# Splitting operands of five matrix products one stage ahead in a fused two-block kernel

## The reference, cut to what matters

```python
def conv_ffn(h, w_up, conv_w, conv_b, w_down):
    u = h @ w_up
    up = jnp.pad(u, ((0, 0), (1, 1), (0, 0)))
    u = up[:, :-2] * conv_w[0] + up[:, 1:-1] * conv_w[1] + up[:, 2:] * conv_w[2] + conv_b
    a, b = jnp.split(u, 2, axis=-1)
    return (jax.nn.silu(a) * b) @ w_down
...
        h = _rms(x, mix_norm_g[l])
        p = h @ w_in[l]
        a_out = _mla(...)
        kf = _hyena_filters(...)
        h_out = _hyena(p[..., OFF_HY:], hy_conv_w[l], hy_conv_b[l], kf, hy_skip[l])
        mixed = jnp.concatenate([_rms(a_out, attn_out_g[l]), _rms(h_out, hy_out_g[l])], axis=-1)
        x = x + mixed @ w_out[l]
        x = x + _mem_xattn(_rms(x, cross_norm_g[l]), _rms(mem, mem_norm_g[l]), w_mq[l], w_mkv[l], w_mo[l])
```

## Time and profile before

| what | value |
|---|---|
| median of 3 runs | 2826.53 us (2824.12 to 2827.61) |
| the profiled execution | 2820.73 us, span 2818.9 us |
| PE busy | 89% of the span |
| DVE, ACT, POOL busy | 49%, 30%, 9% |
| mean granted PE clock | 0.936 of full |

### The profile page before, as it was taken

One profiled execution on the slowest core, in us unless ns is written; L12 is line 12 of the kernel. 1 busy time (PEld: TensorE's weight loads), 2 busy tenths in 40 slices (PEclk: granted clock), 3 DMA queues, 4 the chain that ended last, 5 costly groups with the idle time before them and its releaser, 6 DMA issues. The chain is left out here.

```text
span 2818.9 us, 34789 instructions
## 1 busy us (share of the span) xinstructions
PE 2498.3 (89%) x14602; PEld 1936.7 (69%) x14602; DVE 1390.7 (49%) x2216; ACT 847.1 (30%) x1347; POOL 249.8 (9%) x180
## 2 busy tenths in 40 slices
PE   6997979999997998998799998998785889897887
PEld 5885658888886888985589996756533368573322
DVE  3324554666666115226657775356576645423223
ACT  4223443323224114224533333123401542221001
POOL 0002420000000000004300000000131020011112
PEclk8998989999998999997999998999897999988998
DMA  5114721111120112226322223211101013347996
GB/s 237 60 53 117 272 107 45 60 60 60 61 71 31 62 62 75 75 80 201 117 75 93 96 93 123 94 48 60 56 0 53 0 61 135 120 182 317 425 424 276
DMA packets 53949, 326.89 MB, mean 116 GB/s; under 512 B 7646, under 2 KB 13918, under 8 KB 25950
## 3 DMA queue, kind: packets, MB, share of 16 engines
q1 hardware_dynamic: 40750, 302.76, 28.7%
q0 software_dynamic: 5696, 12.59, 1.2%
q10 hardware_dynamic: 7344, 9.28, 1.0%
HBM read 317.26 MB, written 12.58 MB: 117 GB/s over the span
## 5 line engine op out<-in xcount | busy, mean ns | idle before, releaser
L947 PE MATMUL ps<-work_rounded,ring_rounded 128*128 128x512 f32 (+3 forms) x2128 | 576.3, 356 | 30.3 <-DVE work_rounded L395 13.1
L947 PE MATMUL ps<-xn_rounded,ring_rounded 128*128 128x512 f32 (+2 forms) x2304 | 545.0, 349 | 0.0
L2007 PE MATMUL ps<-xn_rounded,ring_rounded 128*128 128x258 f32 (+2 forms) x2816 | 533.9, 312 | 0.0
L2007 PEld LDWEIGHTS ps<-xn_rounded,ring_rounded 128*128 128x128 f32 x2816 | 413.4, 190 | 31.2
L947 PEld LDWEIGHTS ps<-work_rounded,ring_rounded 128*128 128x128 f32 (+2 forms) x2128 | 359.7, 193 | 92.7 <-DVE work_rounded L395 13.7
L947 PEld LDWEIGHTS ps<-xn_rounded,ring_rounded 128*128 128x128 f32 x2304 | 375.9, 192 | 58.0 <-issue 0.2
L947 PE MATMUL ps<-big_rounded,ring_rounded 128*128 128x512 f32 (+2 forms) x1160 | 337.4, 369 | 52.9 <-DVE big_rounded L854 43.7
L854 DVE TENSOR_TENSOR ring_rounded<-ring,ring_rounded 128x2048 fp32r<-128x2048 f32 (+2 forms) x94 | 189.0, 2015 | 254.5 <-ACT ring_rounded L822 254.4
L2007 PE MATMUL ps<-work_rounded,ring_rounded 128*128 128x256 f32 (+1 forms) x1232 | 279.6, 308 | 9.0 <-PEq L782 4.8
L947 PEld LDWEIGHTS ps<-big_rounded,ring_rounded 128*128 128x128 f32 (+1 forms) x1160 | 205.0, 196 | 95.9 <-DVE ring_rounded L854 32.3
L822 ACT ACTIVATE ring_rounded<-ring 128x2048 fp32r<-128x2048 f32 (+2 forms) x94 | 158.2, 1688 | 357.6 <-PE ps L947 351.7
(11 more groups left out here) (400 smaller groups left out, 3104.5 us busy)
## 6 DMA issues: line engine op xcount, KB each, us to landing
ring<-in_stream SPq DMA_DIRECT2D x141, 1024.0 KB, 4.8
big<-in_experts SPq DMA_DIRECT2D x22, 2048.0 KB, 29.3
ring<-in_stream SPq DMA_DIRECT2D x32, 704.0 KB, 3.9
ring<-in_experts SPq DMA_DIRECT2D x22, 1024.0 KB, 28.8
xn<-in_experts SPq DMA_DIRECT2D x5, 2048.0 KB, 30.4
work<-in_experts SPq DMA_DIRECT2D x5, 2048.0 KB, 35.5
big<-in_first_modulation SPq DMA_DIRECT2D x8, 1024.0 KB, 14.0
work<-in_bias ACTq DMA_DIRECT2D x24, 256.0 KB, 4.4
```

The costliest lines, as they stand in the source:

```text
L947: mm = pe.matmul(out[:, a - u.first:b - u.first], lhs, rhs, start=j == 0 and n == 0 and not u.onto, stop=j == terms - 1 and n == len(passe ...
L2007: mm = pe.matmul(out[:, a:b], ws[:, k, :], x[k][:, a - base:b - base], start=k == 0 and n == 0, stop=k == KT - 1 and n == 2)
```

## The change

Each of the five products gets part of its sources split in the stage before it. `project` takes `tiles_ahead`: the split order and PE's waits then start at that tile.

- `ffn_up` of the last layer splits tiles 0 to 8 of the down projection, one per tile of its own loop (ACT in half 1 of tile i for tile i-2, DVE for tile i-3), and at the last tile the first strip of the down projection. That strip's high part would fall on `high[0]`, which `ffn_up` uses for its own weights, so from here on the parity of the two areas is swapped (`turn`).
- `hyena_filters` splits 5 of the 8 tiles of `second_projection`: ACT after its exponentials, DVE between `take(0)` and `take(1)`. For this the hyena inputs lie in other columns of `work`.
- The latent attention splits the four hyena tiles of `mixed_projection`: ACT in units 10, 14, 18, 22, DVE in the unit behind.
- `mixed_projection` splits the 8 memory tiles of the memory projection: ACT after the square of units 0 to 7, DVE after these units.
- The memory attention splits 6 of the 8 tiles of `output_projection`: two by ACT in each of units 6, 10, 14, DVE in the unit behind.

```diff
+    def high_of(self, n):
+        return self.high[(n + self.turn) % 2][:, 0:WIDTH[n]]
...
-            for k in range(len(sources)):
+            for k in range(tiles_ahead, len(sources)):
...
-                            pe.wait_ge(tile_low.sem, tile_low.at(seen_tiles))
+                            if seen_tiles > tiles_ahead:
+                                pe.wait_ge(tile_low.sem, tile_low.at(seen_tiles - tiles_ahead))
@@ attention, vector and scalar @@
+                    for n, (at_unit, _, value, high) in enumerate(next_tiles):
+                        if u == at_unit + 1:
+                            dve.wait_ge(next_high.sem, next_high.at(n + 1))
+                            self.split_low(dve, value, high)
...
+                    for at_unit, outputs, value, high in next_tiles:
+                        if u == at_unit:
+                            act.wait_ge(stored.sem, stored.at(outputs))
+                            self.split_high(act, value, high).then_inc(next_high.up(), 1)
                     if pair_at(u, 2) is not None:
@@ ffn_up, scalar and vector @@
+                    if c == 1 and 0 <= i - 2 < tiles_ahead:
+                        act.wait_ge(gated.sem, gated.at(len(runs) * (i - 1)))
+                        self.split_high(act, *down_sources[i - 2]).then_inc(next_high.up(), 1)
+                    if (i, c) == (FT - 1, 0):
+                        for number, value, room in views():
+                            self.split_high(act, self.strip(act, number), room).then_inc(next_high.up(), 1)
...
+                    if c == 1 and 0 <= i - 3 < tiles_ahead:
+                        dve.wait_ge(next_high.sem, next_high.at(i - 2))
+                        self.split_low(dve, *down_sources[i - 3])
+                    if (i, c) == (FT - 1, 0):
+                        for _, value, room in views():
+                            dve.wait_ge(next_high.sem, next_high.at(tiles_ahead + 1))
+                            self.split_low(dve, value, room)
@@ hyena_filters, vector and scalar (PAIRED_AHEAD = 5) @@
+                take(0)
+                for k in range(PAIRED_AHEAD):
+                    dve.wait_ge(next_high.sem, next_high.at(k + 1))
+                    norm.low(dve, k)
+                take(1)
...
+                for k in range(PAIRED_AHEAD):
+                    if k == 3:
+                        act.wait_ge(multiplied.sem, multiplied.at(16))
+                    norm.high(act, k).then_inc(next_high.up(), 1)
@@ latent attention @@
+            next_tiles=[(10 + 4 * i, 1, mix[:, 4 + i, :], room) for i, room in enumerate(self.hyena_high())],
@@ mixed_projection @@
+            if i < KT:
+                memory_norm.high(act, i).then_inc(next_high.up(), 1)
...
+        def after(dve, i):
+            if i < KT:
+                dve.wait_ge(next_high.sem, next_high.at(i + 1))
+                memory_norm.low(dve, i)
@@ memory_attention @@
-        self.project(units, 12, finish, sources=rooms, deferred=norm, early=KT)
+        self.project(units, 12, finish, sources=norm.rooms, deferred=norm, early=KT, tiles_ahead=KT)
...
+            next_tiles=[(6 + 4 * (m // 2), 2 * (m // 2) + 2, o[:, m, :], self.output_high[m]) for m in range(6)])
```

More of the change, by code:

```diff
@@ L463, in on_tensor @@
             pe.wait_ge(b.hyena_landed, 64)
-            pe.matmul(b.bank(1)[0:64, :], b.v("w1", 0, 64)[0:33, :], b.work[0:33, 6144:6144 + S], start=True, stop=True).then_inc(self.done.up(), 1)
+            pe.matmul(b.bank(1)[0:64, :], b.v("w1", 0, 64)[0:33, :], b.work[0:33, 10240:10240 + S], start=True, stop=True).then_inc(self.done.up(), 1)
         if i == 4:
@@ L765, in __init__ @@
         self.issued = 0
-        self.ahead = 0
+        self.ahead = self.turn = 0
         self.freed_at = []
@@ L873, in project @@
     def project(self, units, strips, finish, sources, banks_each=1, prefetch=None, deferred=None, add=None, gpsimd=None,
-                early=None, following_strip=False, loads=None, following_halves=False, after=None, beside=None):
+                early=None, following_strip=False, loads=None, following_halves=False, after=None, beside=None, tiles_ahead=0):
         first = len(self.freed_at)
@@ L898, in parts @@
             low_w = [self.rounded(a) for a in slot]
-            high_w = [self.rounded(self.high[(first + s) % 2][:, 0:WIDTH[first + s]]) for s in strips_of_unit]
+            high_w = [self.rounded(self.high_of(first + s)) for s in strips_of_unit]
             low_x, high_x = ([self.rounded(t[part]) for t in sources] for part in (0, 1))
@@ L1005, in split_strip @@
                     else:
-                        ins = self.split_high(act, strip, self.high[(first + s) % 2][:, 0:WIDTH[first + s]])
+                        ins = self.split_high(act, strip, self.high_of(first + s))
                     ins.then_inc(strip_high.up(), 1)
@@ L1984, in ffn_up, with views @@
         halves_of = [(i, c) for i in range(FT) for c in range(2)]
+        down_sources, tiles_ahead = self.down_sources(l, width)
+        next_high = self.sig("next_high")
+        if not need_ctx:
+            self.turn = 1
+        def views():
+            return self.split_ahead(0 if need_ctx else 1)
         with self.stage() as block:
@@ L2090, in _, with down_sources @@
                         gate(i - 1)
+                    if c == 1 and 0 <= i - 3 < tiles_ahead:
[5 more added lines that the diff above has]
+                            self.split_low(dve, value, room)
                 convolve(*halves_of[-1])
                 gate(FT - 1)
+    def down_sources(self, l, width):
+        if l < DEPTH - 1:
+            rooms, ahead = tiles_in(width, self.xn, self.work), 0
+        else:
+            at = (FT + 1) * width
+            rooms = tiles_in(width, self.big[:, at:16384], self.xn, self.big[:, FT * width:at])
+            ahead = (16384 - at) // width
+        return [(self.g[:, k, :], room) for k, room in zip(range(FT), rooms)], ahead
     def ffn_down(self, l, need_ctx):
@@ L2106, in ffn_down @@
         last = l == DEPTH - 1
-        rooms = tiles_in(width, self.xn, self.big[:, FT * width:]) if last else tiles_in(width, self.xn, self.work)
-        self.project(units, 2 * KT, finish, banks_each=2, sources=[(g[:, k, :], room) for k, room in zip(range(FT), rooms)],
+        sources, tiles_ahead = self.down_sources(l, width)
+        self.project(units, 2 * KT, finish, banks_each=2, sources=sources, tiles_ahead=tiles_ahead,
                      following_strip=True, loads=self.load_hyena_inputs if last else None, beside=FilterFeatures(self) if last else None)
@@ L2235, in _ @@
                     combine(o)
-                for o in range(2):
-                    take(o)
+                take(0)
[3 more added lines that the diff above has]
+                take(1)
             @block.scalar
@@ L2254, in second_projection @@
     def second_projection(self):
[L2255 to L2256 removed]
+        p2, norm = self.bigs(0, 16, S), self.pair_norm
         self.p2 = p2
[L2258 to L2261 removed]
         units = []
@@ L2271, in finish, with paired_sources @@
             return eng.tensor_tensor(p2[0:n, i, :], ps, norm.rstd[0:n, :], ALU.mult)
-        self.project(units, 8, finish, sources=rooms, deferred=norm)
+        self.project(units, 8, finish, sources=norm.rooms, deferred=norm, tiles_ahead=PAIRED_AHEAD)
+    def paired_sources(self):
+        xn, w = self.xns(KT, S), self.work
+        rooms = [(w[:, 6144 + k * S:6144 + (k + 1) * S], xn[:, k, :]) for k in range(KT)]
+        areas = tiles_in(S, self.xn[:, 4096:6144])
+        self.first_rstd = w[:, 10240:10752]
+        self.both_gains = self.small[:, 96:104]
+        self.pair_norm = PairNorm(self, rooms, areas[0:2], areas[2:4], areas[1], self.first_rstd)
     def hyena(self):
@@ L2555, in add_squares, with memory_sources @@
                     settle(pool, pool.tensor_tensor(total, total, passes[(m - 1) % 3], ALU.add), added)
-        self.project(units, 4, finish, sources=rooms, deferred=OutputNorm(self, rooms, w[:, 7168:7680]), early=4, add=square, gpsimd=add_squares,
-                     following_strip=True)
+        memory_norm = self.memory_norm = self.memory_sources()
+        self.project(units, 4, finish, sources=rooms, deferred=OutputNorm(self, rooms, w[:, 7168:7680]), add=square, gpsimd=add_squares,
+                     following_strip=True, after=after, tiles_ahead=4)
+    def memory_sources(self):
+        xn, w = self.xns(KT, S), self.work
+        rooms = list(zip(tiles_in(256, self.big[:, 12288:14336]), tiles_in(256, self.big[:, 2048:4096])))
+        rooms += [(w[:, 2048 + k * S:2048 + (k + 1) * S], xn[:, k, :]) for k in range(KT)]
+        return MemoryNorm(self, rooms, self.memory, (self.memory_squares, self.stream_squares), (w[:, 8448:8704], w[:, 8704:9216]), self.small[:, 0:2])
     def memory_attention(self):
-        xn, hm, w = self.xns(KT, S), self.bigs(2048, KT, 256), self.work
```

(7 more changed lines are left out.)

46 lines of the change are left out of this document (24 added, 22 removed).

## The result

The changed kernel took 2806.7 us (median of 4 runs, 2805.9 to 2809.0), the kernel before, on the same chip, 2825.3 us (4 runs, 2824.1 to 2827.6). The ratio is 0.9935, with a 95% interval from 0.992 to 0.995. The gain by the medians is 18.6 us; 17.6 was forecast, and 2806.7 lies in the range and in the forecast's own range.

A forecast was written before the change was run, and what follows sets the result against it. PE, busy 89% of the span, was taken as the bound, standing at block starts for split operands. Gains 9.8 + 3.2 + 0.6 + 3.1 + 0.9 = 17.6 us: 2826.5 - 17.6 = 2808.9, range 2800 to 2818 (own 2804 to 2814).

The forecast's parts named there:

- The down projection: PE starts at about 1716.2, no longer waits for strip 1, and unit 0 ends at 1734.5: gain 9.8 us.
- The second projection: ACT and DVE lose five of eight tiles at its start, so everything behind moves up: gain 3.2 us.
- The mixed projection: Its head gains 3.1 us from wait and clock, four splits in the latent attention lose 2.5: net 0.6.
- rival 1: In the attention loops each of ten tiles delays PE in full: loss 11.4 instead of 4.7, time 2815.6; chance 0.12.
- The memory projection: Eight tiles split earlier let strip 1 and all behind move up: gain 3.1 us, moved work hidden in mixed projection.
- The output projection: Its head gains 3.1 us from wait and clock, six splits in the memory attention lose 2.2: net 0.9.
- The second: Down projection gains only its head, strip 1 or tables being late: 3.7 instead of 9.8, time 2815.0; chance 0.06.
- The third: More is gained: attention tiles cost nothing and the clock stays up: 2803 us or less; chance 0.12.
- The fourth: Whole kernel: no change in time because later waits swallow the gain, 2824 to 2829 us; chance 0.03.
- The fifth: Added waits in the attention loops make PE's clock fall and stay at 1.2 GHz: slower, 2849 us; chance 0.03.

The follow-up runs named there:

- e6: Kernel before's down projection tiles put back into the changed kernel, so only its first strip is split ahead there; other products as changed; 2816.03 us.
- e7: Changed kernel with only the nine tiles of the down projection split ahead, not its first strip; 2810.37 us.
- e10: The changed kernel unaltered, timed and profiled once more; 2809.24 us, ratio 0.994.
- e4: Changed kernel without the down projection's splits in `ffn_up`; the other four products stay split ahead; 2818.17 us, ratio 0.9971.
- e1: Changed kernel with the latent attention's four splits two units later, in units 12, 16, 20, 24; 2808.37 us, ratio 0.9937.
- e5: Changed kernel with splits moved: two each in latent attention units 15 and 23, and memory attention units 7, 11, 14; 2807.02 us, ratio 0.9944.
- e11: Same kernel as e5, run again on another chip, against the changed kernel's split places in both attentions; 2803.88 us, ratio 0.992.
- e12: Changed kernel with only the latent attention's splits moved, two each to units 15 and 23; 2804.22 us, ratio 0.9922.
- e8: Changed kernel without the memory tiles' splits in the mixed projection; 2816.46 us.
- e2: Changed kernel without the splits inside the two attentions, so mixed and output projection split all tiles at their own start; 2808.04 us, ratio 0.9942.
- e3: Changed kernel with only the down projection's nine tiles and first strip split ahead, the other four products as before; 2815.71 us, ratio 0.9964.

## Why the prediction was right

**The down projection** (9.8 forecast) gave 9.96, by both numbers of the working: PE started 6.04 us after the up projection's end (1716.2 - 1710.2 = 6.0 forecast), at half clock, and unit 0 took 18.12 us (18.3): 10.3 for the first 33 matmuls and 7.8 for the others (10.6 and 7.75). The window of its start and one from the end of unit 0 on, changed kernel:

```profile
1720.00:1725.60 5.60, 5.60 (x13) 4.42 (x14) 4.97 (x9) 5.60 (x11) 0.00 (x0) 0.50 0.78 218
...
1737.00:1848.00 111.00, 110.33 (x472) 87.55 (x470) 36.29 (x35) 22.74 (x17) 0.00 (x0) 1.00 0.26 94
```

No wait for strip 1 stands in unit 0, the tables were there, and unit 1 ran at the pace of before. e6 and e7 show the two mechanisms one by one, and e6 that tiles, not strip 0, free the time for strip 1.

**The second projection** (3.2) gave 3.06 to its sum of squares, where PE still waits, 2.40 us. Another 1.16 came behind it: in the changed kernel's profile the granted clock was 0.50 from 1916.9 to 1920.3, ahead of PE's next wait for a strip, which took it in (0.72 us instead of 1.92), and not behind that wait, as from 1940.9 on before. In e10, the same kernel, and in e4 that stretch took 87.45 us as before, so it belongs to the execution, not to the edit.

**The mixed projection** (net 0.6) gave net -0.4: the step that was mis-sized is the loss in the latent attention, 3.3 us (3.0 in e10) instead of 2.5. The head gained 2.9 of 3.1: the pause fell by 1.37 and the clock stayed up, with 15 matmuls in 3.4 us instead of 9.

```profile
2260.10:2263.50 3.40, 3.40 (x15) 2.76 (x16) 3.36 (x2) 0.00 (x0) 0.00 (x0) 1.00 0.01 2
```

In the loop the places were those named: the square's wait went from 0.47 to 0.99 us, and the normalising behind unit 14, in hand before, made a wait of 0.67. These are the 0.5 and 0.7 of the working: twice each is 2.4 (the prediction's sum says 2.5), and all of PE's waits for the squares and the normalising grew by 2.4. The other 0.9 goes with the clock, low for longer than before near the end of the attention (6.8 us from 2248.0, instead of 3.4 from 2258.3). In all seven profiles with these splits in units 10 or 12 and on it was low there for 6.8 us, in the seven others for 3.4; so it goes with the added waits, though how they bring it about isn't shown. What the working did not see is that the loss was a matter of the place in the cycle of eight units (rival 1 speaks of "each fourth unit"), which e1 (no better) and e5, e11 and e12 (loss gone) show.

**The memory projection** (3.1) gave 3.07, and 3.3 by e8. PE's wait at the start shrank by 1.05 us only (these stand in the row of the mixed projection in the table); the wait for strip 2 remained (2.84 us of 5.03), and what moved is everything ahead of it. The splits beside POOL cost DVE 0.91 us instead of 0.41 a tile, 3.4 us over the eight, against the bound of up to 8 x 1.1 (the 1.1 has no source: an add alone took 0.74 in e8). What DVE owes PE behind them, strip 2 behind the first four and strip 3 behind the other four, was split after idle times of 1.84 and 5.39 us. The Trainium skill's rule on the port that DVE and GpSimd share (SBUF — State Buffer, "Who interferes with whom") agrees with the direction: here it about doubles the operation, hidden. (The sentence that the prediction quotes stands in the summary at the end of that page. The add of 2.48 us that it takes for POOL's first is the fourth of the seven.)

**The output projection** (net 0.9) gave 3.1 net, and this is the term that missed most. The head gained 3.24, and 3.1 was forecast, but the agreement is partly luck: the pause shrank by 1.38 us through the splits, and the rest is the clock, which was full at this place in e2 and e3 too, with the pause as before. The memory attention should have grown by 2.2 and grew by 0.13. The waits came where they were put: 0.48 us at 2433.2 (0.5 forecast for unit 6), 1.29 at 2443.95 (1.2 for unit 10), and 0.81 instead of 0.47 ahead of the last values (0.5 for unit 14), 2.1 together. But the last values, eight matmuls, took 3.70 us at full clock (2451.28, above), where they took 5.40 before, in this window of the kernel before:

```profile
2462.40:2467.80 5.40, 5.36 (x8) 1.99 (x8) 0.69 (x2) 0.00 (x0) 0.00 (x0) 0.68 0.00 0
```

The 1.7 us that the clock gave there paid for most of the splits' waits. In all eight profiles with the splits in units 6, 10 and 14 these matmuls took 3.70 us, in the six others 5.3 to 5.4. Against e2 and e3, which split nothing here and start the projection at full clock, attention and head together gain only 1.0 to 1.5 us (0.6 to 1.1 for e10). So of the 3.1 us some 1.6 to 2.1 are no work of these splits; what brought the clock up at the head in every changed kernel is open.

**In the routing** 1.4 us were given back, which no step of the prediction has. The same 36 us of the routing, first of the kernel before:

```profile
2519.90:2555.90 36.00, 25.40 (x164) 24.66 (x164) 15.23 (x75) 8.44 (x10) 3.25 (x3) 0.61 0.71 283
```

and after:

```profile
2503.90:2539.90 36.00, 28.45 (x164) 27.92 (x164) 14.22 (x75) 8.32 (x10) 2.51 (x3) 0.55 0.67 269
```

The number of matmuls is the same, 164, and they are busy for 3.05 us more at a granted clock of 0.55 instead of 0.61. The two profiles of the kernel before took 35.97 and 35.99 us here, the twelve of changed kernels 37.2 to 38.2, e3 among them, which splits nothing ahead behind the down projection. The cause isn't settled: the stage's own work is the same in all. One rival is untested: e3 and all the others keep the changed kernel's places of buffers (the inputs of the filters, the rooms of the split tiles, the squares), and no run moves these back.

**Of the rivals**, none decided. The first (all attention tiles lose in full) would have been 11.4 us in the two loops; they grew by 3.4. The second (only the head) fell by the missing wait. The third is what e11 and e12 come to for the latent attention: its splits can cost nothing. The fourth (no change) fell with the time, 18.6 us lower. The fifth, the clock down for tens of microseconds, did not show: unit 1 of the down projection on and both attentions ran at the pace of before but for stretches of 3 to 7 us. Predicted 17.6, by the stages 18.0, by the medians 18.6: the mixed pair came out 1.0 lower than its term and the output pair 2.2 higher (most of it the clock), the second projection 1.0 more from the clock and the routing 1.4 less. These cancel to 0.8; that the total is so near is partly their luck.

## What to carry to other kernels

When a block starts with the engine that matters waiting for prepared operands, follow its first unit to the last of its waits: the gain is what the last one moves by, and here the operands that freed the way to it were worth more than those it starts with. Extra work in a software-pipelined loop belongs in front of the long idle time of the engine that does it, and behind what the other engine waits for there; here the same instructions cost nothing at that place, and 3.3 us at two other placings in the cycle. Check first how many units the loop's cycle really has. Compare two traces stage by stage and not by their spans, and keep apart what the clock gives or takes in one execution. A variant that leaves one part of the change out tells what that part is worth better than the kernel before does: beside it, the output pair's 3.1 us became 1.0 to 1.5.

## What the runs showed of the hardware

- A pause of PE of 2.5 us before a block's start was followed by half clock in the kernel before and by full clock in e2 and e3 (output projection); at the mixed projection's start it was followed by half clock in e2 too. Behind pauses of 1.1 us the clock was full in the changed kernel. What decides beside the pause is open.
- A DVE operation of 128x256 with two operands in SBUF took 0.41 us alone and 0.91 beside POOL's adds (each from its start to the next one's). A POOL add of that size took 0.74 us alone, 0.80 beside such an operation and 2.48 when DVE's split of a 128x2048 strip, 2.29 us long, had begun before it.
- The part up to the down projection, common to all but for the splits in the second layer's `ffn_up`, ended (last matmul of the up projection) at 1710.2 and 1711.0 us in the two profiles of the kernel before, and at 1712.5 to 1718.5 in the twelve of changed kernels; the routing was 1.2 to 2.2 us longer in them. The same work, and in the places compared above at a lower granted clock. Why is open.
